# Attention by pairs of heads, one per half of the partitions, and no zero matmuls in any attention stage of a two-block kernel

## The chip, the cores and the metric

The kernel runs on one core of one Trainium2 chip. The metric is the device time of one execution, in microseconds (us). Everything is float32; weights and activations of the large products are split into a high and a low part (type fp32r), and each product is three matmuls.

## The reference

Two blocks over a sequence of 256 tokens and width 1024 (`D_MODEL`). The first: swiglu FFN, short convolution, FFN, shared keys and values, FFN, sparse attention (`nsa_mixer`), FFN. The second: an even mixer and an odd mixer. The three attention stages that the change touches:

```
# nsa: 16 heads of 64, in 4 groups; three branches per head
s_c = q @ k_c.T * scale + bias        # 15 compressed keys
p_c = masked_softmax(s_c); o_c = p_c @ v_c
s_s, o_s = ...  # selected blocks: with 256 tokens all 4 blocks are selected
s_w, o_w = ...  # window of 512: all causal keys
out = g0 * o_c + g1 * o_s + g2 * o_w; return out @ w_o
# even: 8 heads of 64 over the 64 best keys of each query (dsa_attention), beside 4 heads of retention
# odd: 4 differential heads (softmax map 1 minus lambda times map 2, 64 wide each, values 128 wide),
#      a norm over their output, beside 8 latent heads (keys 96 wide, values 64 wide)
```

## The kernel before, in words

The activations lie transposed, feature by token: `qT[:, i]` has the queries of heads 2i (partitions 0 to 63) and 2i+1 (partitions 64 to 127) for 256 tokens. An attention stage is a list of *maps*, one per head and branch. A full map is 128 x 384: queries 128 to 255 against all 256 keys in columns 0 to 255, queries 0 to 127 against 128 keys in columns 256 to 383. A compressed map ("cmp") is 128 x 30. The list of nsa has 48 maps, for each pair of heads three of the lower head, then three of the upper one; even has 8, odd 16.

`attend(name)` stands once per engine, and the copies meet by semaphores. In step `st`:
- TensorE (lines 821 to 877) makes the scores of map `st` into one of three banks (L834, L835; L838, L839 for cmp), transposes map `st - LAG` once it is scaled (L852 to L854), and multiplies map `st - LAG - 1` with the values (L870, L871; L873 for cmp), with `LAG = 5`. In nsa, `fill=2` adds two matmuls of zeros to each step, 128 x 512, into a bank that nobody reads (L876).
- VectorE adds the bias (L1722), takes the row maxima (L1724, L1725), and, one step later, inverts the sums of the exponentials (L1739), applies the gates (L1740) and scales a third of the map (L1745). When a tile of the output is complete, it evacuates it and splits it into `hnh` and `hnl` (L1562, L1563).
- ScalarE copies the transposed map out (L1314) and makes the exponentials with their sums (L1325).
- GpSimd scales the other 256 columns (L2139). In nsa it also loads the diagonals of the bias for the next pair.

`NP_ = 7` maps may be in flight. Each stage is followed by the output projection `mix_out`: 8 chunks of 24 matmuls (L643 to L645), one per tile, after its opening (L656) and a wait for the last tile (`mix_ready`). Its weight chunks pass through a ring of two: SP loads one when the low part of the chunk two before is done, ScalarE makes the high part (`hi_b`, L1114), and the low part is made by GpSimd for chunks 0 and 1 (`lo_b`, L2067), ahead of `attend`, and by VectorE for the others (`mix_rest`, L1767), behind it.

Ahead of nsa, `project("q")` makes the queries in four chunks of 256 columns and the gates in a last chunk of 48. Each chunk of queries is normed: squares on ScalarE, sums on TensorE (L606), root on ScalarE (L1147), `normed_queries` on VectorE (L1491, a reciprocal of 128 x 512, and L1847). In the odd stage the differential heads are normed in the same way (`c_norm`: L1491, L2036, L2037, L1562, L1563), each pair of tiles at a step chosen by `C_DONE`. The nsa stage has its own step counts: the bias diagonals of a pair are awaited by VectorE at its first map.

Of the kernel before, what the change touches and what calls it, by code (L numbers as in the profile page):

```python
# [17 lines left out]
F32 = mybir.dt.float32  # L18
# [7 lines left out]
P = 128  # L26
T = 256
# [5 lines left out]
NP_ = 7  # L33
LAG = 5
# [67 lines left out]
def build(nc, a, out):  # L102
    ctx = ExitStack()
    with ctx:
# [48 lines left out]
        pbuf = sb("pbuf", [P, NP_, 384])  # L153
        ptb = sb("ptb", [P, 2, 384])
        nmx = sb("nmx", [P, NP_, 2])
        sm = sb("sm", [P, NP_, 2])
        rs = sb("rs", [P, NP_, 2])
# [7 lines left out]
        bank = [ctx.enter_context(nc.psum_tensor(f"bank{i}", [P, 512], F32)) for i in range(8)]  # L165
# [139 lines left out]
        Q_COLS = [(T * c, T) for c in range(4)] + [(1024, 48)]  # L305
# [27 lines left out]
        NPAR, NGAIN = len(PARAMS), 6  # L333

# [6 lines left out]
        def _(sp):  # L341
# [65 lines left out]
            def load_rows(w):  # L407
                v = kmaj(w)
                for c in range(KT):
# [22 lines left out]
            load_rows(a["attn_w_o"][0])  # L432
# [5 lines left out]
            load_rows(a["w_out_even_2"][0])  # L438
            load_cols(odd_w, ODD_COLS)
            load_rows(a["w_out_odd_2"][0])  # L440
# [28 lines left out]
        def special(chunk, parts, moves):  # L469
# [5 lines left out]
            "q": [fm(c, qT[:, 2 * c:2 * c + 2]) for c in range(4)] + [nat(4, 0, 48, gates[:, :, :], ACT.Sigmoid)],  # L475
# [44 lines left out]
        def full(q, k, bias, scale, v, rows, coef=None):  # L520
            return dict(kind="full", q=q, k=k, bias=bias, scale=scale, v=v, rows=rows, coef=coef)

        def nsa_units():
            units = []
            for pair in range(8):
                maps = []
                for h in (2 * pair, 2 * pair + 1):
                    half, g = 64 * (h % 2), h // 4
                    r = slice(half, half + 64)
                    q = qT[r, pair]  # L530
                    maps.append(dict(kind="cmp", q=q, k=kcT[r, g * NC:(g + 1) * NC],
                                     bias=tcmp[:, :].rearrange("p (i n h) -> p h i n", i=2, h=16)[:, h],
                                     scale=SQRT_D, v=vc[:, g * 64:(g + 1) * 64], rows=(half, 64),
                                     coef=gates[:, :, 3 * h]))
                    for br in range(2):
                        src = kT if (g % 2) * 64 == half else kS
                        maps.append(full(q, src[r, 2 * br + g // 2], t384[:, pair % 2, h % 2, :], SQRT_D,
                                         [vn[:, br, t, g * 64:(g + 1) * 64] for t in range(2)], (half, 64),
                                         coef=gates[:, :, 3 * h + 1 + br]))
                units.append((maps, pair, None))  # L540
            return units

        def even_units():
            units = []
            for pair in range(4):
                maps = []
                for h in (2 * pair, 2 * pair + 1):
                    half = 64 * (h % 2)
                    r = slice(half, half + 64)
                    maps.append(full(eq[r, pair], ek[r, pair], dmask, SQRT_D,  # L550
                                     [ev[:, t, h * 64:(h + 1) * 64] for t in range(2)], (half, 64)))
                units.append((maps, pair, eg[:, pair]))
            return units

        def odd_units():
            units = []
# [1623 lines left out]
```

## Time and profile before

| | us |
|---|---|
| median of 3 runs | 1516.56 (1515.64 to 1526.63) |
| profiled execution, time | 1513.4 |
| its span | 1511.2 |
| mean granted clock of TensorE | 0.951 of 2.4 GHz |
| busy: TensorE, VectorE, ScalarE, GpSimd | 1402.4, 911.8, 629.7, 438.7 |

The span is what the profile shows from the first to the last instruction of the execution, 2.2 us less than its time. The busy time of an engine is the time in which at least one of its instructions was under way. In the timeline an fp32 matmul shows as two records (x2), whose modelled ends overlap the next instruction; the start-to-start distance is what it costs.

### The profile page before, as it was taken

The numbers are of one execution on the slowest core, as the hardware profiler recorded it, in microseconds if no ns is written. First come the engines' busy times: TensorE is split into PE (matmuls) and PEld (weight loads), VectorE is DVE, ScalarE is ACT, GpSimd is POOL, SyncE is SP. The second block draws the span as 40 slices with busy tenths as digits, with TensorE's granted clock in tenths as the row PEclk, the third lists the DMA queues.
The fourth block names the chain that finished last, engine by engine and source line by source line (L and its number), as shares of the span: only waits on it lengthen the run. The fifth ranks groups of instructions, "written<-read, shape, count | busy, mean of one in ns | idle before, by whom it ended". The sixth has DMA issues, their size and how long they took to land.

```text
span 1511.2 us, 27677 instructions
## 1 busy us (share of the span) xinstructions
PE 1402.4 (93%) x10817; PEld 1288.6 (85%) x10817; DVE 911.8 (60%) x1424; ACT 629.7 (42%) x953; POOL 438.7 (29%) x226
## 2 busy tenths in 40 slices
PE   5999999989999999999979999999999979799766
PEld 4999999989999989999955557899999977688646
DVE  3685468875455665454665664745557695573764
ACT  3344343344334454343434553533443443434442
POOL 1344431214443253434114440344330012000310
PEclk8999999999999999999977999999999997899788
DMA  7768745658766466565430002665644531353002
GB/s 203 216 187 239 213 127 176 189 161 243 217 187 193 127 188 207 178 196 167 130 113 21 22 22 74 206 194 183 206 139 129 165 128 47 105 164 112 28 1 84
DMA packets 271772, 222.53 MB, mean 147 GB/s; under 512 B 8082, under 2 KB 252326, under 8 KB 271580
## 3 DMA queue, kind: packets, MB, share of 16 engines
q1 hardware_dynamic: 268176, 212.44, 46.3%
q0 software_dynamic: 2368, 7.60, 2.2%
q10 hardware_dynamic: 1164, 1.62, 0.3%
q8 instruction: 42, 0.69, 0.2%
q14 instruction: 22, 0.18, 0.0%
HBM read 216.40 MB, written 4.19 MB: 146 GB/s over the span
## 4 chain that ended last, share of the span: by engine, by line
PE 76%; DVE 14%; ACT 5%; DMA 3%; issue 2%; ACTq 0%; DVEq 0%; SPq 0%
PE bank L643 21%; PE bank L645 20%; PE bank L644 20%; DVE wal L1509 2%; PE bank L834 2%; PE bank L876 2%; PE bank L870 2%; DVE rstd L1491 2%; ACT wah L1107 1%; DVE hnl L1527 1%; PE bank L852 1%; ACT hnh L1175 1%; DVE wal L1683 1%; PE bank L835 1%; DMA raw_a<-in_ffn_w_in 1%
## 5 line engine op out<-in xcount | busy, mean ns | idle before, releaser
L643 PE MATMUL bank<-hnh,wah 128*128 128x256 f32 (+1 forms) x2080 | 590.8, 284 | 12.5 <-DVE wal L1509 5.7
L2067 POOL TENSOR_TENSOR wbl<-raw_b,wbh 128x1024 fp32r<-128x1024 f32 x102 | 338.7, 3322 | 878.6 <-ACT wbh L1114 765.2
L644 PE MATMUL bank<-hnl,wah 128*128 128x256 f32 (+1 forms) x2080 | 582.9, 280 | 0.0
L645 PE MATMUL bank<-hnh,wal 128*128 128x256 f32 (+1 forms) x2080 | 582.4, 280 | 0.0
L643 PEld LDWEIGHTS bank<-hnh,wah 128*128 128x128 f32 (+1 forms) x2080 | 397.4, 191 | 18.9 <-issue 10.4
L644 PEld LDWEIGHTS bank<-hnl,wah 128*128 128x128 f32 (+1 forms) x2080 | 395.9, 190 | 2.0 <-issue 1.4
L645 PEld LDWEIGHTS bank<-hnh,wal 128*128 128x128 f32 (+1 forms) x2080 | 396.2, 190 | 0.0
L1509 DVE TENSOR_TENSOR wal<-raw_a,wah 128x2048 fp32r<-128x2048 f32 (+1 forms) x129 | 298.2, 2312 | 95.0 <-ACT wah L1107 93.6
L1107 ACT ACTIVATE wah<-raw_a 128x2048 fp32r<-128x2048 f32 (+3 forms) x127 | 238.9, 1884 | 98.5 <-PE bank L645 80.7
L643 PE MATMUL bank<-hidh,wbh 128*128 128x256 f32 x768 | 214.6, 279 | 4.6 <-DVE hidl L1563 4.5
L1213 ACT ACTIVATE gate_hid<-tmp 128x256 f32<-128x256 f32 x88 | 36.7, 417 | 429.3 <-DVE tmp L1618 429.3
L644 PE MATMUL bank<-hidl,wbh 128*128 128x256 f32 x768 | 214.1, 279 | 0.0
L645 PE MATMUL bank<-hidh,wbl 128*128 128x256 f32 x768 | 214.0, 279 | 0.0
L1618 DVE TENSOR_TENSOR tmp<-bank,rms 128x512 f32<-128x512 f32 x88 | 60.8, 691 | 221.7 <-PE bank L645 214.3
L643 PEld LDWEIGHTS bank<-hidh,wbh 128*128 128x128 f32 x768 | 146.0, 190 | 5.3 <-DVE hidl L1563 4.9
L1114 ACT ACTIVATE wbh<-raw_b 128x1024 fp32r<-128x1024 f32 x120 | 125.2, 1046 | 60.2 <-PE bank L645 37.2
L645 PEld LDWEIGHTS bank<-hidh,wbl 128*128 128x128 f32 x768 | 145.4, 189 | 0.0
L644 PEld LDWEIGHTS bank<-hidl,wbh 128*128 128x128 f32 x768 | 145.3, 189 | 0.0
L2139 POOL TENSOR_SCALAR pbuf<-pbuf,rs 128x256 f32<-128x256 f32 (+1 forms) x72 | 63.9, 887 | 87.4 <-DVE rs L1740 63.0
L1325 ACT ACTIVATE pbuf<-pbuf,nmx 128x128 f32<-128x128 f32 (+2 forms) x144 | 59.4, 413 | 41.6 <-DVE nmx L1725 35.8
L1622 DVE TENSOR_TENSOR gate_hid<-gate_hid,tmp 128x256 f32<-128x256 f32 x88 | 39.5, 448 | 42.7 <-ACT gate_hid L1213 42.7
L834 PE MATMUL bank<-arena 64*128 64x256 f32 (+1 forms) x112 | 46.6, 528 | 18.0 <-DVEq L1968 8.4
(245 smaller groups left out, 1758.7 us busy)
## 6 DMA issues: line engine op xcount, KB each, us to landing
raw_a<-in_ffn_w_in SPq DMA_DIRECT2D x176, 512.0 KB, 5.1
raw_b<-in_ffn_w_out SPq DMA_DIRECT2D x88, 512.0 KB, 4.8
raw_a<-in_w_in_even SPq DMA_DIRECT2D x15, 1024.0 KB, 5.3
raw_a<-in_conv_w_in SPq DMA_DIRECT2D x24, 512.0 KB, 4.2
raw_a<-in_w_in_odd SPq DMA_DIRECT2D x11, 1024.0 KB, 5.3
raw_a<-in_w_kv SPq DMA_DIRECT2D x6, 1024.0 KB, 5.8
raw_b<-in_conv_w_out SPq DMA_DIRECT2D x8, 512.0 KB, 5.8
raw_a<-in_attn_w_q SPq DMA_DIRECT2D x4, 1024.0 KB, 5.3
```

The costliest lines, as they stand in the source:

```text
L643: mm(dst, wh, xh, start=start, stop=False)
L644: mm(dst, wh, xl, start=False, stop=False)
L645: return mm(dst, wl, xh, start=False, stop=stop)
L834: mm(b[:, 0:T], m["q"][:, P:T], m["k"], start=True, stop=True)
L1107: act.activation(wah[:, s, :, 0:w], raw_a[:, wa.slot(u), :, 0:w], ACT.Copy).then_inc(S("a_hi"), 1)
L1114: act.activation(wbh[:, s], raw_b[:, s], ACT.Copy).then_inc(S("b_hi"), 1)
L1325: x = act.activation(pbuf[:, r, lo:hi], pbuf[:, r, lo:hi], ACT.Exp, bias=nmx[:, r, i:i + 1], accum_out=sm[:, r, i:i + 1])
L1509: v.tensor_tensor(wal[:, s, :, 0:w], raw_a[:, (n["ra"] + u) % 2, :, 0:w], wah[:, s, :, 0:w].bitcast(F32), ALU.subtract).then_inc(S("a_lo"), 1)
L1618: v.tensor_tensor(tmp[:, gs, :].rearrange("p (g c) -> p g c", g=2), bank[4 + gs][:, :].rearrange("p (g c) -> p g c", g=2), rln[:, None, :] ...
L1622: link(v.tensor_tensor(hf[:, hs, :], silu[:, gs, :], tmp[:, gs, T:2 * T], ALU.mult))
L2067: g.tensor_tensor(wbl[:, s], raw_b[:, s], wbh[:, s].bitcast(F32), ALU.subtract).then_inc(S("b_lo"), 1)
L2139: g.tensor_scalar(pbuf[:, r, lo:hi], pbuf[:, r, lo:hi], rs[:, r, 1:2], None, ALU.mult).then_inc(S("p1_scaled"), 1)
```

## The change

Two maps of the two heads of a pair become one *duo*, which passes all engines as one step: nsa 24 duos (cmp, full, full per pair of heads), even 4, odd 8. The scores of the two heads go to two neighbouring banks, alternating between the halves of the partitions (in the odd stage's differential heads the two halves are the two maps of one head; the latent heads have 96 partitions each, from 0 on). VectorE and ScalarE handle both maps in one instruction where they can, by a view over two banks; ScalarE's exponentials and GpSimd's scaling stay one per map. Values of a duo alternate between the halves of the output's partitions. At most 3 duos are in flight, and `LAG` is 2.

The two zero matmuls per step are gone. The gates' chunk of `project("q")` moves from last to second. The norms of the last two query chunks move into the nsa stage on VectorE, in halves of 256 columns at steps 2, 4, 6 and 8, with TensorE's sum of the last one at its step 1 and its waits at steps 12 and 18. GpSimd's low parts of chunks 0 and 1 move behind `attend` in all three stages; in nsa ScalarE's two high parts move to its steps 14 and 15. `mix_out` waits for each tile (`tile_ready`) in place of the last one, and takes tiles 4 to 7 first in even and odd. In odd both norms of the differential heads move to VectorE's end: `c_norm(0)` in step 10, `c_norm(1)` behind `attend`, their sums at TensorE's steps 8 and 9.

```diff
-NP_ = 7
-LAG = 5
+ND = 3
+LAG = 2
...
+def two_banks(i, rows, w):
+    return psum[0:rows, 512 * i:512 * (i + 2)].rearrange("p (b c) -> p b c", b=2)[:, :, 0:w]
-Q_COLS = [(T * c, T) for c in range(4)] + [(1024, 48)]
+Q_COLS = [(0, T), (1024, 48)] + [(T * c, T) for c in range(1, 4)]
+OUT_ORDER = {"nsa": list(range(8)), "even": [4, 5, 6, 7, 0, 1, 2, 3], "odd": [4, 5, 6, 7, 0, 1, 2, 3]}
+TILE_COUNT = {"nsa": {c: c + 1 for c in range(8)}, "even": {c: 8 + c + 1 for c in range(4)},
+              "odd": {4: 13, 5: 14, 6: 15, 0: 16, 1: 16, 7: 17, 2: 18, 3: 18}}
@@ TensorE @@
-    def mix_out():
+    def mix_out(name):
+        pe.wait_ge(S("rt_ready"), n["rn"])
         open_acc()
+        for i, c in enumerate(OUT_ORDER[name]):
+            if c in TILE_COUNT[name]:
+                pe.wait_ge(S("tile_ready"), TILE_COUNT[name][c])
+            add_rows(i // 2, i % 2, hnh[:, c, :], hnl[:, c, :], KT)
...
+                x0 = 2 * (g % 2)
+                if g >= 2:
+                    pe.wait_ge(S("max_ready"), g - 1)
+                if du["kind"] == "full":
+                    for i in range(2):
+                        mm(bank[x0 + i][:, 0:T], q[i][:, P:T], k[i], start=True, stop=True)
+                    for i in range(2):
+                        x = mm(bank[x0 + i][:, T:384], q[i][:, 0:P], k[i][:, 0:P], start=True, stop=True)
...
+                if du["kind"] == "full":
+                    pe.wait_ge(S("p1_scaled"), fulls(name, j))
+                if g >= 1:
+                    pe.wait_ge(S("pt_copied"), g)
+                for i in range(2):
+                    p, b = pbuf[:, 2 * (g % ND) + i], bank[6 + i]
+                    if du["kind"] == "full":
+                        pe.transpose(b[:, 0:P], p[:, T:384], ident)
...
+                elif rows[0] == rows[1]:
+                    for i in range(2):
+                        mm(o[:, 0:T], v_[i][0], pt[i][:, 0:T], start=i == 0, stop=False)
+                        x = mm(o[:, P:T], v_[i][1], pt[i][:, T:384], start=False, stop=i == 1)
                 else:
+                    for i in range(2):
+                        mm(o[rows[i], 0:T], v_[i][0], pt[i][:, 0:T], start=first, stop=False)
+                    for i in range(2):
+                        x = mm(o[rows[i], P:T], v_[i][1], pt[i][:, T:384], start=False, stop=last)
-                    for _ in range(fill):
-                        mm(bank[6][:, :], zero[:, 0:P], zero[:, :], start=True, stop=True)
...
-    attend("nsa", fill=2)
-    pe.wait_ge(S("mix_ready"), 1)
-    mix_out()
+    def nsa_between(st):
+        if st == 1:
+            sum_squares(1, 512, blk1)
+        elif st == 2:
+            pe.wait_ge(S("rt_ready"), n["rn"])
+        elif st in (12, 18):
+            pe.wait_ge(S("late_queries"), st // 6 - 1)
...
+    def sum_heads(st):
+        if st in (8, 9):
+            pe.wait_ge(S("max_ready"), DBASE["odd"] + 7)
+            sum_squares(1, 512, one1, (sqs[:, :], tmp[:, 0, :])[st - 8], bank[st - 8])
@@ ScalarE @@
-    take_root(512, 1.0 / 64)
-    mix_first()
-    attend("nsa")
+    take_root(512, 1.0 / 64, sqs, 1)
+    attend("nsa", lambda st: hi_b(0, st - 14) if st in (14, 15) else None)
@@ VectorE @@
+                if du["kind"] == "full":
+                    link(v.scalar_tensor_tensor(pbuf[:, r, :], two_banks(x0, P, 384), du["scale"], du["bias"],
                                                 ALU.mult, ALU.add))
+                    v.reduce_max(nmx[:, r, 1], pbuf[:, r, 0:T], AX, negate=True)
+                    v.reduce_max(nmx[:, r, 0], pbuf[:, r, T:384], AX, negate=True).then_inc(S("max_ready"), 1)
...
+                    split(hnh[:, tile, :], hnl[:, tile, :], dst).then_inc(S("tile_ready"), 1)
...
+    def late_queries(st):
+        if st in (2, 4, 6, 8):
+            j, t = 1 + (st + 2) // 4, (st // 2 + 1) % 2
...
+            link(v.reciprocal(rstd[:, 0:T], (rt if j == 2 else sqs)[:, t * T:(t + 1) * T]))
+            x = v.scalar_tensor_tensor(qT[:, 2 * j + t, :], qT[:, 2 * j + t, :], gq[:, 0:1], rstd[:, 0:T],
+                                       ALU.mult, ALU.mult)
...
+    attend("odd", behind=lambda st: c_norm(0) if st == 10 else None)
+    c_norm(1)
@@ GpSimd @@
+            if du["kind"] == "cmp":
+                if 1 <= du["unit"] < 7:
+                    diagonals(du["unit"] + 1)
+                continue
+            for r in (2 * (g_ % ND), 2 * (g_ % ND) + 1):
+                x = g.tensor_scalar(pbuf[:, r, 0:T], pbuf[:, r, 0:T], rs[:, r, 1:2], None, ALU.mult)
+            x.then_inc(S("p1_scaled"), 1)
     def mix(name):
+        attend(name)
         for u in range(2):
             lo_b(0, u)
-        attend(name)
```

## Rows read from the trace of the kernel before

**Rows 1.** The page's chain of work that ended last, by engine.
```profile
PE 76%; DVE 14%; ACT 5%; DMA 3%; issue 2%; ACTq 0%; DVEq 0%; SPq 0%
```

**Rows 2.** Stretches: length, busy us of PE, PEld, DVE, ACT, POOL; PEclk; DMA share.
```profile
774.90:788.70 13.80, 4.25 (x6) 1.10 (x5) 10.28 (x5) 6.84 (x9) 4.64 (x2) 0.50 0.12 39
788.70:811.40 22.70, 22.70 (x62) 12.00 (x62) 10.48 (x42) 8.15 (x35) 5.82 (x8) 0.50 0.07 23
811.40:918.70 107.30, 106.53 (x529) 58.53 (x527) 65.80 (x254) 54.26 (x205) 42.44 (x53) 1.00 0.08 23
1245.10:1265.20 20.10, 19.25 (x60) 12.97 (x61) 15.30 (x44) 9.71 (x37) 10.13 (x9) 0.50 0.17 53
1428.50:1449.50 21.00, 16.52 (x98) 13.35 (x97) 17.14 (x44) 14.07 (x42) 7.55 (x8) 0.99 0.00 0
```

**Rows 3.** Timeline of PE in nsa: start, length, line, forms, count [idle before].
```profile
844.79 0.61 PE L876 MATMUL bank<-zero 128*128 128x512 bf16 x2
845.33 0.70 PE L834 MATMUL bank<-arena 64*128 64x256 f32 x2
...
846.17 0.33 PE L852 MATMUL bank<-cst,pbuf 128*128 128x128 f32 x1
...
846.65 0.65 PE L870 MATMUL bank<-ptb,arena 128*64 128x256 f32 x2
847.13 0.38 PE L871 MATMUL bank<-ptb,arena 128*64 128x128 f32 x2
847.45 0.60 PE L876 MATMUL bank<-zero 128*128 128x512 bf16 x2
...
852.61 0.70 PE L834 MATMUL bank<-arena 64*128 64x256 f32 x2
```

**Rows 4.** Timeline of PE, first scores of even and of odd.
```profile
1245.12 1.23 PE L834 MATMUL bank<-arena 64*128 64x256 f32 x4 [8.45 <-DVEq L1968]
1246.10 0.68 PE L835 MATMUL bank<-arena 64*128 64x128 f32 x4
...
1412.26 1.23 PE L834 MATMUL bank<-arena 64*128 64x256 f32 x4 [7.96 <-DVEq L2024]
```

**Rows 5.** Timeline of PE, last value products of even.
```profile
1269.34 0.38 PE L871 MATMUL bank<-ptb,arena 128*64 128x128 f32 x2
1269.51 0.65 PE L870 MATMUL bank<-ptb,arena 128*64 128x256 f32 x2
```

**Rows 6.** Timeline of the other engines in nsa.
```profile
824.42 0.56 DVE L1722 SCALAR_TENSOR_TENSOR pbuf<-bank,t 128x384 f32<-128x384 f32 x1 [0.30 <-PE bank L835]
825.01 0.42 DVE L1724 TENSOR_REDUCE nmx<-pbuf 128x1 f32<-128x256 f32 x1
825.35 0.28 DVE L1725 TENSOR_REDUCE nmx<-pbuf 128x1 f32<-128x128 f32 x1
825.54 0.16 DVE L1739 RECIPROCAL rs<-sm 128x2 f32<-128x2 f32 x1
...
828.32 0.51 ACT L1325 ACTIVATE pbuf<-pbuf,nmx 128x256 f32<-128x256 f32 x1 [0.54 <-DVE nmx L1725]
828.64 1.02 POOL L2139 TENSOR_SCALAR pbuf<-pbuf,rs 128x256 f32<-128x256 f32 x1 [0.58 <-DVE rs L1740]
```

**Rows 7.** Timeline ahead of nsa.
```profile
785.74 2.58 DVE L1847 SCALAR_TENSOR_TENSOR arena<-arena,par,rstd 128x512 f32<-128x512 f32 x1
...
788.70 0.60 PE L838 MATMUL bank<-kcT,arena 64*128 64x15 f32 x2 [8.26 <-DVEq L1862]
```

**Rows 8.** Timeline around the openings of the output projections of nsa and odd.
```profile
918.69 1.04 PE L656 MATMUL bank<-zero 128*128 128x512 bf16 x4 [0.77 <-DVE hnl L1563]
...
1458.29 3.35 DVE L1491 RECIPROCAL rstd<-rt 128x512 f32<-128x512 f32 x1 [0.19 <-ACT rt L1147]
...
1464.38 0.42 DVE L1756 TENSOR_TENSOR arena<-bank,arena 128x256 f32<-128x256 f32 x1
...
1466.76 1.89 PE L656 MATMUL bank<-zero 128*128 128x512 bf16 x4 [5.29 <-DVE hnl L1563]
```

More of the change, by code:

```diff
@@ L513, in wait_finished, with nsa_duos @@
                 eng.wait_ge(S("job_finished"), BY_ACT[jobs])
[L520 to L524, printed above, removed]
+        def nsa_duos():
+            duos = []
             for pair in range(8):
[L526 to L541, printed above, removed]
@@ new lines, in nsa_duos @@
+                for br in range(2):
+                    src = [kT if (g % 2) == half else kS for half in range(2)]
+                    duos.append(dict(kind="full", q=q, k=[src[i][rows[i], 2 * br + g // 2] for i in range(2)],
+                                     bias=t384[:, pair % 2, :, :], scale=SQRT_D,
+                                     v=[[vn[:, br, t, g * 64:(g + 1) * 64] for t in range(2)]] * 2, rows=rows,
+                                     coef=gate[1 + br], first=False, last=br == 1, **tile))
@@ new lines, in nsa_duos, with even_duos @@
+            return duos
+        def even_duos():
+            duos = []
+            rows = [slice(0, 64), slice(64, P)]
+            for pair in range(4):
+                duos.append(dict(kind="full", q=[eq[r, pair] for r in rows], k=[ek[r, pair] for r in rows],
+                                 bias=dmask[:, None, :].to_broadcast([P, 2, 384]), scale=SQRT_D,
+                                 v=[[ev[:, t, h * 64:(h + 1) * 64] for t in range(2)] for h in (2 * pair, 2 * pair + 1)],
+                                 rows=rows, coef=None, first=True, last=True, tile=pair, unit=pair, gate=eg[:, pair]))
+            return duos
@@ L562, in odd_units @@
             for pair in range(4):
-                maps = []
-                for h in (2 * pair, 2 * pair + 1):
-                    maps.append(full(q96[0:96, h], k96[0:96, h], causal, 96 ** -0.5,
-                                     [mv[:, t, h * 64:(h + 1) * 64] for t in range(2)], (64 * (h % 2), 64)))
-                units.append((maps, 4 + pair, dg[:, pair]))
-            return units
-        STAGES = {"nsa": nsa_units(), "even": even_units(), "odd": odd_units()}
-        C_DONE = 8 + LAG + 1
@@ L572, in build @@
[L572 to L587 removed]
+                hs = (2 * pair, 2 * pair + 1)
@@ new lines, in odd_duos @@
+                duos.append(dict(kind="full", q=[q96[0:96, h] for h in hs], k=[k96[0:96, h] for h in hs], bias=bias,
+                                 scale=96 ** -0.5, v=[[mv[:, t, h * 64:(h + 1) * 64] for t in range(2)] for h in hs],
+                                 rows=rows, coef=None, first=True, last=True, tile=4 + pair, unit=4 + pair,
+                                 gate=dg[:, pair]))
+            return duos
+        STAGES = {"nsa": nsa_duos(), "even": even_duos(), "odd": odd_duos()}
@@ L866, in attend @@
+                        o, v_, first, last = bank[4 + gu % 2], du["v"], du["first"], du["last"]
+                        pt = [ptb[:, 2 * (g % 2) + i] for i in range(2)]
                         pe.wait_ge(S("pt_copied"), g + 1)
```

347 lines of the change are left out of this document (167 added, 180 removed).

## The prediction, made before the change was run

> **What bounds the kernel now.** I read the chain that ended last first: TensorE holds 76% of it, VectorE 14% [rows 1]. Then the busy time by stretches, for the clock and for how full TensorE is around the three attention stages [rows 2]. In the first one (nsa, 8 pairs of heads, 48 maps) TensorE is busy 106.5 of 107.3 us, always at the full 2.4 GHz, while VectorE, ScalarE and GpSimd have 66, 54 and 42 us of work there. So the stage is as long as TensorE's instruction stream. Before it stand 13.8 us with little on TensorE and 22.7 us at half clock (1.2 GHz), in which every record of it is twice as long. The timeline gives the stream's parts, start to start [rows 3]: the scores of a full map 0.84 us (845.33 to 846.17), three transposes 0.48, the two value products 0.80, the two zero matmuls 0.54 (844.79 to 845.33). Three steps (one compressed map, two full ones) repeat after 7.28 us (845.33 to 852.61), a pair of heads after 14.57, eight pairs after 116.6. The zero matmuls are 6 x 0.54 = 3.2 us of each pair, 26 us of the stage.
>
> **What the change takes off TensorE.** Zero matmuls: those 3.2 us per pair. Scores of a pair: one head has partitions 0 to 63, the other 64 to 127, and two maps on different halves do run side by side: at the start of the even stage four records of 256 columns and four of 128 belong to two maps and take 1245.12 to 1246.78, 1.66 us at half clock [rows 2, 4], where two maps one after the other would need 4 x 0.84 = 3.4. So a pair's scores cost 0.84 at full clock; in the last four units of the odd stage, with 96 partitions, they stay at 1.68. Value products of a pair: the heads write different halves of the output's partitions. The trace has one place where such products follow each other with nothing between: the second product of one head starts at 1269.34 and the first of the next head at 1269.51 [rows 5], 0.17 later, where inside the nsa stage the next instruction comes 0.32 after it (847.13 to 847.45) [rows 3]. They overlapped, so I take 0.8 for a pair; the other end is 1.6, nothing shared. The Trainium skill, "TensorE: Matmul & The Clock Gate", section "Measured speedup vs the span model", has 2.38 times for three column tiles; by that a pair would take about 0.9 to 1.0 (an estimate from that page). The row agrees in kind. Transposes use the whole array and stay, 0.96 per pair.
>
> **What is late next.** TensorE's work per nsa pair falls to about 2.2 (scores) + 2.5 (transposes) + 2.2 (values) = 6.9 us. What sets the pace then is a ring through all engines, since only three pairs of maps are in flight (ND = 3, LAG = 2) where seven maps were. Its other terms [rows 6]: on VectorE one map takes 0.56 + 0.42 + 0.28, 1.12 to the reciprocal's start; doubling the elements from 128 to 256 costs 0.14, so a fixed 0.14 of each operation is saved by handling two maps at once: 0.98 + 0.70 + 0.42, less the overlap that these operations show, 1.92 for a pair. Reciprocal and multiplication about 0.37. GpSimd scales 256 columns in 1.02, twice: 2.04. ScalarE: four exponentials, about 1.84.
> Over one unit (three steps) TensorE's program order and the waits close this ring: transposes 0.96, values 0.80, scores 0.84, VectorE's scores-to-maximum 1.92, factor 0.37, GpSimd 2.04, transposes 0.96, values of the compressed maps 0.57 (estimated between 0.48 and 0.80 [rows 3]), scores 0.84. Sum 9.3, and 0.3 for three or four hand-overs: 9.6 us per pair of heads, against 14.57. Eight: 77. The new waits are these: TensorE waits for GpSimd's scaling with the next values and scores queued behind it, and VectorE waits behind those scores with the factors of the maps before.
>
> **Stage by stage,** on the profiled execution (span 1511.2, time 1513.4):
> - Gap before nsa. The projection ends where the first stretch begins [rows 2], 774.9, and the first score is at 788.70 [rows 7], behind two query norms on VectorE and a blocked one: 2.58 us at 785.74, while GpSimd made a low part. The last two norms move into the stage as eight small operations (about 8.6 us on VectorE, which has room) and GpSimd's work moves to its end. Left: one sum of squares, an evacuation, about 2.3 us. The 48-column chunk moves from last to second; the clock was already at half where it ended [rows 2], and now full-width matmuls follow it: 1.7 lost. First score at 778.9.
> - nsa. First scores and their root 2 us, 77, then the drain of the last pair: maximum 1.9, exponentials 1.8, factor, GpSimd 2.0, transposes 1.0, the copy of 768 columns 0.9 (estimated), values 0.8, hand-overs: 9.7; opening the banks 0.9. That is 90. The start-up has holes of 4 to 5 us on TensorE, after which I expect half clock until the pipe is full: 5 us. First product of the output projection at 873, where it was about 0.7 behind the opening at 918.69 [rows 8], 919.4. Gain 46.
> - even. Four pairs are hardly a pipe: the last scores about 9 behind the first, drain 9.7: 19 us at full clock, 23 at half; it starts cold again, so 21.5, against 25.2 (1245.12 to 1270.3) [rows 4, 5]. The wait of about 0.8 ahead of the mix [rows 8] goes, and GpSimd no longer blocks VectorE at the start, about 1.8. Gain 6.
> - odd. Without compressed maps the ring closes over two steps: 0.96 + 1.6 (values of full width share nothing) + 0.84 + 1.92 + 0.37 + 2.04 = 7.7, later 7.8 (values 0.8, scores 1.68), with hand-overs 4.1 a pair. Last scores at 28, drain 9.7: 38, cold start plus 4: 42, against 49.2 (1412.26 [rows 4] to 1466.76 less 5.29 idle [rows 8]). Then both head norms, 6.1 us each (1458.29 to 1464.38 [rows 8]), stand on VectorE behind the last evacuations, ahead of the low parts of chunks 2 to 7. The mix starts at once with two chunks (5.4 us) and then waits about 8, where it waited 5.3 ahead; and the clock may drop: 1.5. Gain 7 - 2.7 - 1.5 = 3.
> - Moved loads. SP may refill a weight buffer only behind GpSimd's low part, now at the end of each stage. GpSimd makes the first one (4.64 us for two [rows 2], 2.3) while TensorE does the last transposes and values (about 3), so I cost it at nothing; if VectorE's port use stretches these to 3.5, each stage gives back up to 1 to 3 us.
> Sum: 46 + 6 + 3 = 55 to 56. 1513.4 - 55.7 = 1457.7. The median of the runs shown, 1516.56, is 3.2 above the profiled execution; most of that I expect again: **1460**.
>
> **The rivals.**
> 1. *Half clock through nsa.* For it: the even stage stayed at 0.50 for 20 us with TensorE busy 19.25 of 20.10, and without zero matmuls; nsa took 22.7 us to reach full clock even with them [rows 2]. Against: from 1428.5 to 1449.5 the odd stage holds 0.99 with TensorE busy only 79%, no zero matmuls in it. The ring's TensorE terms double, 4.97 to 9.9, and a unit takes 9.6 + 5.0 = 14.6, as long as now: 8 x 5.0 = 40 less the 5 already in. 1495, and up to 1507 if the odd stage stays cold too.
> 2. *The value products do not overlap.* For it: one place only shows overlap. The ring gets 0.8 + 0.57 longer, 11.0 a unit: 11 us in nsa, 2 or 3 in the others. 1473.
> 3. *Slower than before.* Both at once: value products one after the other and half clock. TensorE alone then needs 2 x (2.2 + 2.5 + 4.3) = 18 us per pair, where the forecast has 9.6: 8 x 8.4 = 67, less the 5 already in, and about 12 in the other two stages: 1534. It turns slower than before where a pair passes about 16.
> 4. *Scores do not pair up in the steady stage,* because transposes and values stand between: of the two places that show the overlap neither is in such a step [rows 4]. 2 x 0.84 a unit more, and 2 us in even and odd each: about 1475.
> 5. *VectorE alone sets the pace,* the ring's waits being hidden. Its work in a unit is 2 x (1.92 + 0.37 + 0.45 for scaling) + 1.0 for the compressed maps + 1.2 for the output tile, both estimated from operations of that size [rows 6]: 7.7 against the ring's 9.6. Eight units are 15 us less: 1445. The Trainium skill, "TensorEngine Tiling (Array Packing)", section "PSUM Bottleneck", says that tiling speeds up TensorE but not the emptying of PSUM, which may then be the bound. By that rule it would be this case; the rows have VectorE at 66 us of 107 [rows 2], and no more than 62 of the 77 to come.
>
> **How the numbers follow.** Forecast 0.58 (own range 1446 to 1473), half clock 0.2, rival 2 0.09, rival 4 0.03, slower 0.06, rival 5 0.04. The range reaches from 1441 to 1497, which leaves out the slow case and the far end of rival 1. Faster by over 1% (15 us, about what a measurement here can tell from no change): 0.90. Within 1%: 0.04. Slower: 0.06.
>
> **What would show it.** A period of 9.6 us between the first scores of two pairs in nsa; score records of two heads with starts closer than 0.2 us, and value records likewise; TensorE waiting for GpSimd's scaling as its largest wait in the stage, not VectorE; a gap of 2 to 3 us ahead of nsa; in the odd mix a hole of about 8 us after two chunks, released by VectorE. Granted clock 1.0 in most of nsa. Wrong would make it: 0.50 there, one of the rings through ScalarE (copy of 768 columns ahead of the exponentials) being longer than mine, or diagonals that land late (3.2 us, now asked for three steps ahead of use, not six).

## The result, and the profile after

| kernel | time, us (median; lowest to highest) | profiled execution, its span |
|---|---|---|
| before | 1516.1 (1515.4 to 1526.6) | 1513.4, 1511.2 |
| after | 1465.6 (1459.9 to 1472.9) | 1472.9, 1471.2 |

The ratio is 0.9649, with a 95% interval of 0.9603 to 0.9695: 50.5 us less, where 56 were forecast. The profiled execution of after is the longest of its four, 40.5 us under that of before, and the difference by stages says why. Each mark is a start in TensorE's timeline: last product of a projection, first score, opening of the banks, the zero matmul that closes a product. The *mix* is the output projection behind an attention stage.

| stage, us | before | after | difference |
|---|---|---|---|
| start to the end of the first feed-forward | 215.7 | 220.6 | +5.0 |
| convolution | 97.4 | 96.8 | -0.6 |
| second feed-forward | 187.4 | 192.8 | +5.5 |
| keys and values, third feed-forward | 240.7 | 239.3 | -1.4 |
| query projection | 33.6 | 37.9 | +4.3 |
| wait before the first score of nsa | 13.9 | 1.8 | -12.1 |
| nsa, first score to the opening of the mix | 130.0 | 102.9 | -27.1 |
| its output projection, fourth feed-forward, even projection | 317.7 | 318.8 | +1.1 |
| even: wait, attention, mix | 60.3 | 52.4 | -7.9 |
| odd projection and tail | 125.7 | 126.4 | +0.7 |
| odd: wait, attention, mix | 88.9 | 81.4 | -7.5 |

The query projection, the wait, nsa, even and odd together gave 50.3 us. The output projection of nsa, whose low parts the change moves too, is 0.8 us longer (24.7 against 24.0). The +10.5 in two feed-forwards is not the change's work: in a feed-forward the matmuls start either every 0.113 or every 0.118 us (355 or 342 in 40 us), from its first to its last. Stretches of before and of after, with the columns of [rows 2]:
```profile
60.00:100.00 40.00, 40.00 (x355) 40.00 (x354) 31.35 (x41) 14.76 (x18) 18.89 (x8) 1.00 0.72 213
```
```profile
60.00:100.00 40.00, 40.00 (x342) 40.00 (x341) 32.09 (x43) 15.74 (x18) 18.86 (x8) 1.00 0.73 217
```
Granted clock and busy time are the same. Over the 14 profiles of this study the first feed-forward has the slow pitch in 7, the second in 4, the third in all 14 (before too), the fourth in 2. A slow one is longer by about 6 us (6.1, 6.6 and 6.5 on average in the first, second and fourth), so the time of one execution moves by that much without any edit; below, stage lengths are compared beside the medians.

Stretches of after; the first, seventh and eighth answer to [rows 2], the second to fifth are pieces of a single pair of heads:
```profile
789.30:892.20 102.90, 75.04 (x483) 50.36 (x485) 71.04 (x182) 59.98 (x222) 43.94 (x46) 0.73 0.09 25
836.00:840.00 4.00, 1.45 (x18) 1.21 (x17) 3.33 (x13) 1.86 (x8) 2.72 (x3) 1.00 0.22 86
840.00:846.80 6.80, 6.80 (x35) 4.44 (x34) 3.39 (x9) 4.52 (x18) 2.67 (x4) 0.50 0.04 7
846.80:850.30 3.50, 2.15 (x24) 1.33 (x22) 3.08 (x8) 1.73 (x6) 0.79 (x1) 0.99 0.42 104
850.30:857.00 6.70, 5.49 (x24) 3.75 (x24) 3.67 (x10) 4.57 (x15) 3.13 (x4) 0.50 0.00 0
764.00:772.00 8.00, 8.00 (x40) 8.00 (x40) 3.10 (x3) 4.82 (x7) 0.00 (x0) 0.51 0.22 78
1217.60:1238.60 21.00, 15.12 (x88) 11.02 (x90) 15.21 (x31) 11.86 (x38) 11.53 (x10) 0.64 0.03 5
1379.70:1416.30 36.60, 29.45 (x181) 23.17 (x183) 28.29 (x62) 25.78 (x79) 18.43 (x18) 0.86 0.00 1
```
Here the granted clock goes up and down within each pair: 1.00 for some 4 us, 0.50 for some 6.8, then 0.99, then 0.50. Before, once it was up it stayed at 1.00 to the end of nsa. The fifth, sixth and seventh pair take 12.3, 11.7 and 12.3 us between first scores, not 9.6. The timeline of TensorE through one of them answers to [rows 3]:
```profile
833.80 0.70 PE L846 MATMUL psum<-arena 64*128 64x256 f32 x4
834.34 0.39 PE L848 MATMUL psum<-arena 64*128 64x128 f32 x4
834.65 0.28 PE L870 MATMUL psum<-cst,pbuf 128*15 128x128 f32 x1
...
835.19 0.65 PE L892 MATMUL psum<-ptb,arena 128*64 128x256 f32 x4
835.68 0.39 PE L894 MATMUL psum<-ptb,arena 128*64 128x128 f32 x4
836.00 0.62 PE L852 MATMUL psum<-kcT,arena 64*128 64x15 f32 x8
839.17 0.30 PE L866 MATMUL psum<-cst,pbuf 128*128 128x128 f32 x1 [2.55 <-issue]
...
840.93 1.23 PE L846 MATMUL psum<-arena 64*128 64x256 f32 x4
```
Scores of two heads take 0.85 us from start to start (833.80 to 834.65), values of two 0.81 (835.19 to 836.00). Then TensorE is idle for 2.55 us, and 0.8 us after it resumes its records are twice as long. What it waits for, in the waits of TensorE in nsa (us, times, longest):
```profile
PE psum L866 <- issue: 16.5, 7, 2.6
PE psum L866 <- POOL pbuf L2195: 8.8, 3, 5.0
```
"Issue" stands here where TensorE awaited several semaphores (`pt_copied`, `p0_scaled`, `p1_scaled`). GpSimd's two scalings of the duo end at 839.07, and TensorE goes on at 839.17. The timeline of GpSimd:
```profile
837.17 1.90 POOL L2195 TENSOR_SCALAR pbuf<-pbuf,rs 128x256 f32<-128x256 f32 x2 [1.64 <-DVE rs L1773]
```

In the odd stage's output projection, timeline of TensorE, then of VectorE, then of GpSimd:
```profile
1433.98 0.55 PE L651 MATMUL psum<-hnh,wbh 128*128 128x256 f32 x1 [11.24 <-DVE wbl L1807]
```
```profile
1413.48 2.29 DVE L1592 CAST hnh<-arena 128x256 fp32r<-128x256 f32 x1
1415.80 2.47 DVE L1593 TENSOR_TENSOR hnl<-arena,hnh 128x256 fp32r<-128x256 f32 x1
...
1418.64 0.29 DVE L1592 CAST hnh<-arena 128x256 fp32r<-128x256 f32 x1
1418.97 0.43 DVE L1593 TENSOR_TENSOR hnl<-arena,hnh 128x256 fp32r<-128x256 f32 x1
1419.32 3.35 DVE L2085 RECIPROCAL rstd<-rt 128x512 f32<-128x512 f32 x1
...
1426.52 3.35 DVE L2085 RECIPROCAL rstd<-sqs 128x512 f32<-128x512 f32 x1
...
1432.61 2.35 DVE L1807 TENSOR_TENSOR wbl<-raw_b,wbh 128x1024 fp32r<-128x1024 f32 x2
```
```profile
1413.26 4.73 POOL L2122 TENSOR_TENSOR wbl<-raw_b,wbh 128x1024 fp32r<-128x1024 f32 x2
```
The hole is there, 11.2 us. The first two rows of VectorE are a split that takes 0.29 and 0.43 a little later (1418.64); they lie beside GpSimd's two low parts. Beside GpSimd's scalings, which read one tile and not two, the same cast takes 0.30 and the same subtraction 0.50 (nine times in this trace). The kernel before has one such case too: 2.57 and 2.72 us from 1242.22 on, ahead of its even stage.

### The profile page after: what moved, and what is told of

It is laid out like the page before. It is cut to its first block, busy times and chain, and to the rows that moved or that the text cites. A ratio compares the mean times of both kernels' runs of the same rounds, so it can differ in the third digit from the quotient of the medians.

```text
span 1471.2 us, 27135 instructions
## 1 busy us (share of the span) xinstructions
PE 1336.7 (91%) x10692; PEld 1268.2 (86%) x10709; DVE 895.5 (61%) x1260; ACT 617.9 (42%) x915; POOL 428.7 (29%) x210
## 4 chain that ended last, share of the span: by engine, by line
PE 73%; DVE 15%; ACT 5%; issue 3%; DMA 3%; POOL 0%; ACTq 0%; DVEq 0%; SPq 0%; POOLq 0%
PE psum L651 22%; PE psum L653 21%; PE psum L652 21%; DVE wal L1539 2%; PE psum L846 1%; ACT wah L1136 1%; ACT hnh L1206 1%; DVE pbuf L1751 1%; PE psum L866 1%; DVE hnl L1557 1%; DVE wal L1713 1%; DMA raw_a<-in_ffn_w_in 1%; DVE rstd L1521 1%; PE psum L627 1%; DVE rms L1529 1%
## 5 line engine op out<-in xcount | busy, mean ns | idle before, releaser
L651 PE MATMUL psum<-hnh,wah 128*128 128x256 f32 (+1 forms) x2080 | 593.4, 285 | 32.1 <-DVE hnl L1557 13.5
L652 PE MATMUL psum<-hnl,wah 128*128 128x256 f32 (+1 forms) x2080 | 585.0, 281 | 0.0
L653 PE MATMUL psum<-hnh,wal 128*128 128x256 f32 (+1 forms) x2080 | 584.6, 281 | 0.0
L651 PEld LDWEIGHTS psum<-hnh,wah 128*128 128x128 f32 (+1 forms) x2080 | 396.4, 191 | 19.5 <-issue 11.5
L653 PEld LDWEIGHTS psum<-hnh,wal 128*128 128x128 f32 (+1 forms) x2080 | 397.8, 191 | 0.0
L652 PEld LDWEIGHTS psum<-hnl,wah 128*128 128x128 f32 (+1 forms) x2080 | 395.1, 190 | 2.2 <-issue 1.7
L1136 ACT ACTIVATE wah<-raw_a 128x2048 fp32r<-128x2048 f32 (+2 forms) x127 | 238.7, 1882 | 92.9 <-PE psum L653 68.1
L651 PE MATMUL psum<-hidh,wbh 128*128 128x256 f32 x768 | 215.6, 281 | 5.3 <-DVE hidl L1593 5.3
L653 PE MATMUL psum<-hidh,wbl 128*128 128x256 f32 x768 | 215.3, 280 | 0.0
L652 PE MATMUL psum<-hidl,wbh 128*128 128x256 f32 x768 | 215.3, 280 | 0.0
L651 PE MATMUL psum<-hnh,wbh 128*128 128x256 f32 x192 | 55.7, 290 | 13.7 <-DVE wbl L1807 13.6
```

The lines of the kernel that those rows point to most:

```text
L651: mm(dst, wh, xh, start=start, stop=False)
L652: mm(dst, wh, xl, start=False, stop=False)
L653: return mm(dst, wl, xh, start=False, stop=stop)
L1136: act.activation(wah[:, s, :, 0:w], raw_a[:, wa.slot(u), :, 0:w], ACT.Copy).then_inc(S("a_hi"), 1)
```

## The experiments

All start from the kernel after, but e8. "nsa" is the stretch from its first score to the opening of its mix, as in the table. Behind each median stands the ratio to the kernel before, which ran again beside each group of runs with medians from 1512.1 to 1519.0. So a gain over after is a little uncertain where it is taken from medians of different groups: e1, e2 and e12 are 23, 20 and 33 us below 1465.6 by the medians, but some 20, 15 and 29 by the ratios.

**e1: four duos in flight.**
```
-ND = 3, LAG = 2
+ND = 4, LAG = 3      # the fourth place lies in gate_hid, or tmp in the even stage
```


> One more duo in flight in every attention stage: four places for probabilities in place of three, and transposes three steps behind the scores in place of two. The first theory (each unit of the first stage is held by a ring: exponentials, reciprocal, GpSimd's 2 us of scaling, transposes, ScalarE's copy, and ScalarE's next exponentials stand behind that copy) expects the 2.6 us wait of TensorE in each unit to vanish, the granted clock to stay at full and the unit to fall from 12 us to 8 to 9 us: 20 to 28 us less than the changed kernel's 1465.6, so about 1440. The rival that the half clock would come anyway, because TensorE has too little to do between its waits, expects a unit of 11 us or more and under 8 us of gain. The rival that VectorE or GpSimd by itself sets the pace expects no gain.

1442.5 us (1437.2 to 1446.6), ratio 0.9517 (0.9453 to 0.9582). 23 us less, as expected; but nsa gave 16 of them (86.9 us), even 1.2 and odd 5.2. The pairs take 4.8, 14.7, 8.3, 14.9, 6.8, 11.1 and 6.6 us, between first scores. Stretches: nsa, and its first two pairs:
```profile
778.10:865.00 86.90, 67.16 (x482) 44.98 (x484) 70.99 (x182) 59.25 (x222) 44.01 (x46) 0.81 0.11 32
778.10:797.60 19.50, 13.71 (x80) 8.90 (x80) 15.40 (x33) 11.82 (x47) 5.05 (x6) 0.65 0.00 1
```
The ring was a cause. That the clock would stay full did not come true: 0.81 on average.

**e2: zero matmuls where TensorE waits.**
```
 pe.wait_ge(S("pt_copied"), g)   # stood behind the other waits; now ahead of the zeros
+for _ in range(20):          # nsa, ahead of the second duo's transposes
+    mm(bank[6][:, T:2 * T], zero[:, 0:P], zero[:, 0:T], start=True, stop=True)
 pe.wait_ge(S("p0_scaled"), g + 1)
```


> Twenty zero matmuls of 256 columns (2.1 us at full clock) put where TensorE waits longest in each unit of the first stage, ahead of the transposes of the second duo of three; nothing else is changed. The first theory (that wait is what takes the clock to half for some 6.5 us of each 12 us unit) expects full clock through the stage, a unit of 9.5 to 10.3 us and 12 to 18 us off 1465.6. The rival that the clock's dips have another cause expects them to stay, and the time unchanged or longer by up to 2 us a unit.

1445.7 us (1438.7 to 1454.4), 0.9548 (0.9481 to 0.9616). nsa 86.4. Stretches of this run: nsa, then the fifth and the sixth pair:
```profile
776.50:862.90 86.40, 77.59 (x642) 55.04 (x644) 70.51 (x182) 60.12 (x222) 42.94 (x46) 0.94 0.10 29
818.20:827.40 9.20, 8.92 (x82) 6.51 (x80) 7.81 (x23) 6.95 (x28) 5.37 (x7) 1.00 0.14 43
827.40:836.70 9.30, 9.02 (x84) 6.57 (x82) 7.91 (x24) 8.69 (x30) 5.46 (x7) 1.00 0.20 45
```
With the same ring, and only zeros added to the work, the last pairs have full clock and take 9.2 us each. So the zeros gave 16.5 us of nsa back, and what they changed is the clock: 0.94 on average against 0.73. The second, third and fourth pair, beside VectorE's late query norms, took 12.8, 12.1 and 10.1.

**e3: both.**
```
 e1, and range(6) ahead of the transposes of both full duos
```


> Both together: four duos in flight, and six zero matmuls of 256 columns ahead of the transposes of each full duo of the first stage. If the longer ring alone ends the wait and the dips, this is no faster than it and up to 8 us slower (12 x 0.107 us in each of 8 units at most 10 us of work). If the dips stay with the longer ring alone, this one takes them away, and comes out 5 to 15 us ahead of it.

1443.2 us (1442.2 to 1448.2), 0.9511 (0.945 to 0.9571); nsa 88.6 at a clock of 0.85. That is no gain over e1, so the 5 to 15 us expected for the case that e1's dips stay did not come. Three late pairs take 7.8, 9.3 and 7.8 us at full clock, but the two in which VectorE has late query norms 16.2 and 15.6. The last two of the three, and the last alone:
```profile
836.30:853.40 17.10, 15.68 (x147) 11.50 (x144) 15.39 (x44) 15.45 (x57) 10.60 (x12) 1.00 0.16 43
845.60:853.40 7.80, 7.80 (x74) 5.75 (x72) 6.96 (x22) 6.93 (x28) 5.30 (x6) 1.00 0.09 17
```
In the pair of 7.8 us TensorE is busy all the time, 1.3 us of it with twelve zero matmuls (an estimate from 12 x 0.107 us), while VectorE and ScalarE are busy for 6.9 to 7.0. The same pair in e1, without zeros:
```profile
838.70:845.30 6.60, 6.60 (x62) 4.66 (x62) 5.76 (x18) 5.83 (x27) 5.04 (x6) 1.00 0.01 2
```
There too TensorE is busy all the time and the clock is full, so in these pairs the zeros cost what they take. Over the three pairs little changes, 24.5 us in e1 (6.8, 11.1, 6.6) and 24.9 here: the pair in between, whose clock in e1 is 0.85, gains what its neighbours lose.

**e4: the order within a pair.**
```
-for i in range(2): mm(... [:, 0:T] ...)      # 256 columns of both heads
-for i in range(2): mm(... [:, T:384] ...)    # then 128 of both
+for i in range(2): mm(...); mm(...)          # one head, then the other; values too
```


> The same matmuls as in the changed kernel, but each head's two score matmuls one after the other, then the other head's, and the same for the values, so that no two of different halves follow each other but at the change of head. The theory that the two halves overlap (a pair of scores in 0.85 us, a pair of values in 0.81 us, where one after the other they would take some 1.5 us each) expects each duo to take 1.3 us more of TensorE, 28 full duos 36 us in all, of which what TensorE's waits now hide is given back: 10 to 30 us slower than 1465.6. The rival that overlap brings nothing because the ring sets the pace expects under 5 us.

1460.5 us (1455.5 to 1476.4), 0.961 (0.9547 to 0.9672): no difference from after. It was no test of the overlap. Timeline of TensorE, this run:
```profile
841.01 0.71 PE L846 MATMUL psum<-arena 64*128 64x256 f32 x4
841.55 0.39 PE L847 MATMUL psum<-arena 64*128 64x128 f32 x4
841.87 0.28 PE L869 MATMUL psum<-cst,pbuf 128*15 128x128 f32 x1
```
Issued as 256, 128, 256, 128 columns, they still ran as both 256 and then both 128, in 0.86 us (the first two rows are four records each; the first of the two heads start 0.013 us apart): the second head starts beside the first even if another matmul of the first stands ahead of it in the kernel. The trace does not show where on the way from the kernel to the engine the order changes. The Trainium skill, "TensorE: Matmul & The Clock Gate", section "The mechanism", has matmuls start strictly in program order; by that only the first head's matmul of 128 columns and the second head's of 256 could lie side by side, and the scores of a duo would take some 1.4 us (an estimate from the rows: 0.54 + 0.54 + 0.32). The row differs, and it decides.

**e5: the heads' scores held apart.**
```
 for i in range(2):
+    if i: mm(bank[x0][:, 384:392], zero[:, 0:P], zero[:, 0:8], start=True, stop=True)
     mm(...); x = mm(...)
```


> The heads' scores held apart: both matmuls of the first head, a zero matmul over all 128 rows with 8 columns, then both of the second head. In the run with the order changed alone the second head's first matmul still started 0.013 us after the first head's, so the order had undone nothing; the full-row matmul should. The theory that pairs are worth their overlap expects a duo's scores to take some 1.75 us in place of 0.85 at full clock, in all three stages, and the time 8 to 22 us over 1465.6 (20 to 28 us if none of it is hidden by waits). The rival that TensorE's waits hide it expects under 4 us.

1502.4 us (1493.3 to 1508.5), 0.9884 (0.9802 to 0.9965): 37 us over after by the medians (36 by the ratios), more than either end. Timeline, at half clock:
```profile
855.48 1.22 PE L848 MATMUL psum<-arena 64*128 64x256 f32 x2
856.50 0.63 PE L849 MATMUL psum<-arena 64*128 64x128 f32 x2
857.06 0.19 PE L847 MATMUL psum<-zero 128*128 128x8 bf16 x1
857.18 1.22 PE L848 MATMUL psum<-arena 64*128 64x256 f32 x2
858.20 0.63 PE L849 MATMUL psum<-arena 64*128 64x128 f32 x2
858.76 0.47 PE L867 MATMUL psum<-cst,pbuf 128*128 128x128 f32 x1
```
3.28 us for a duo, 1.64 at full clock against 0.85. For 16 full duos that is 12.6 us, but nsa grew by 25.2 (to 128.1), and the clock's mean there fell from 0.73 to 0.62. The attention of even grew by 3.3, that of odd by 3.5. So without the overlap the stage has more to do on TensorE and a lower clock besides. What the values' overlap is worth no run shows.

**e6: the normalisations further back.**
```
-attend("odd", behind=c_norm(0) at step 10); c_norm(1); mix_rest()
+attend("odd"); mix_rest with c_norm(0) behind chunk 2, c_norm(1) behind chunk 4
```


> The last stage's two normalisations of the differential heads moved behind the third and the fifth chunk of the output weights on VectorE, in place of ahead of all of them; the same work. The theory that the 11.2 us hole in the last output projection is VectorE's queue (two normalisations of 6.1 us ahead of the third chunk's low half) expects the hole to fall to two of 2 to 4 us, the projection from 36.6 us to 29 to 33, and the time 4 to 7 us under 1465.6. The rival that the hole comes from the transfer or from ScalarE's high half expects it to stay.

1453.9 us (1451.8 to 1455.2), 0.9566 (0.95 to 0.9632); by the profiles the odd mix went from 36.6 to 30.8. What is left of the hole, timeline of TensorE:
```profile
1418.00 0.36 PE L651 MATMUL psum<-hnh,wbh 128*128 128x256 f32 x1 [4.15 <-DVE wbl L1809]
...
1426.36 0.36 PE L651 MATMUL psum<-hnh,wbh 128*128 128x256 f32 x1 [0.95 <-DVE wbl L1809]
```
VectorE's queue it was. The mix explains 5.8 us of the 11.7 by which the median is below 1465.6, where 4 to 7 were expected; the rest has no counterpart in the stages that the edit touches.

**e7: the gates' 48 columns last.**
```
-Q_COLS = [(0, T), (1024, 48)] + [(T * c, T) for c in range(1, 4)]
+Q_COLS = [(T * c, T) for c in range(4)] + [(1024, 48)]
```


> The 48 columns of the gates back in the last place of the query projection. The theory that the chunk in second place costs by the clock (about 8 us of half clock in the projection, 36 to 38 us against 33.6 before) expects the projection 2 to 4 us shorter, the first scores' wait 1 to 3 us longer (sigmoid and gates are then late) and the half clock carried into the first steps of the attention: the time within 3 us of 1465.6 either way. If the wait before the first scores goes back to 8 us or more, the place of the chunk was what shortened it.

1459.9 us (1454.5 to 1466.7), 0.9599 (0.953 to 0.9667), 5.7 us under after, where at most 3 were expected; the ranges overlap, so the medians alone do not tell the two apart. The projection took 33.6 us, the wait before the first score 2.2, nsa 103.0. Over all profiles: 36.2 to 37.9 with the chunk in second place (8 of them), 33.3 to 34.2 with it last (6). Its place costs 2 to 4.6 us, and of the shorter wait at most 0.4 us hangs on it.

**e8: before, without its zero matmuls.**
```
-attend("nsa", fill=2)
+attend("nsa")
```


> The kernel before, with the two zero matmuls of each step of its first attention stage left out and nothing else. The theory that the fill kept the clock up in the changed kernel's twelve-microsecond units too, and that its removal cost there, expects here as well dips of the granted clock wherever TensorE waits over 2 us. In the kernel before the engine waits little between its steps (14.6 us a unit, TensorE busy), so the likeliest is a gain of 5 to 20 us over 1516 from the removed work (48 steps x 2 x 0.21 us); if the clock falls to half for good parts of the stage, it is slower by up to 20 us.

1547.3 us (1541.9 to 1550.5), 1.0177 (1.0102 to 1.0251): slower by 34 than the kernel before as it ran beside it (1513.5). nsa took 162.5 us, against 130.0. Stretches of nsa in this run:
```profile
795.40:957.90 162.50, 161.02 (x481) 96.81 (x482) 75.97 (x296) 61.21 (x240) 48.33 (x60) 0.51 0.07 18
840.00:850.00 10.00, 10.00 (x30) 5.94 (x30) 5.01 (x20) 3.52 (x15) 2.54 (x3) 0.50 0.00 0
```
TensorE is busy 161.0 of 162.5 us, with less to do than in [rows 2], and stays at 1.2 GHz until its last few us (0.77 over the last 7.9). Taken alone, the second half of the change is a loss.

**e9: the fill of e2 on a quarter of the array.**
```
+mm(bank[6][0:64, T:2 * T], zero[0:64, 0:64], zero[0:64, 0:T], ...)   # 20 times
```


> The fill of the second run once more, twenty zero matmuls of 256 columns in the same place, but each over 64 rows and 64 columns of the array, a quarter of it, in place of the whole. TensorE is busy for the same time. The theory that the clock follows how long TensorE is busy expects the result of the whole-array fill: full clock, a unit of 9.2 us, about 1446. The theory that work on the whole array is wanted (the kernel before without its zero matmuls was busy 10.0 of 10 us with single heads on half the rows and stood at half clock from end to end) expects the dips of the changed kernel to stay and a unit of 12 us or a little more: 1460 to 1475.

1459.1 us (1458.0 to 1461.8), 0.9627 (0.9568 to 0.9685); nsa 92.7, between after (102.9) and e2 (86.4). Stretches:
```profile
820.00:830.00 10.00, 8.13 (x38) 5.47 (x40) 5.45 (x17) 5.77 (x25) 5.10 (x6) 0.52 0.01 3
840.00:850.00 10.00, 9.66 (x86) 7.21 (x88) 8.61 (x23) 9.40 (x34) 6.17 (x8) 1.00 0.16 41
```
The last pairs run at full clock in 9.2 us as in e2, but a dip stays around 820 to 830 (a pair of 15.4). Neither theory is borne out as it stands: here the clock stayed up in the last pairs but dropped once where e2's had not. One profile does not say more.

**e10 and e11: what helped, together.**
```
 e1 + e3's fill + e6 + e7, and ahead of the scores of steps 4, 6, 8, 10:
+pe.wait_ge(S("pt_copied"), d0 + st - LAG)
+for _ in range({4: 28, 6: 12, 8: 16, 10: 16}[st]): mm(bank[6] ...)
 e11: also 44 and 56 zero matmuls after the even and the odd projection
```


> Four duos in flight, six zero matmuls ahead of each full duo's transposes and 28, 12, 16 and 16 at the four steps that VectorE's late query normalisations delay, the gates' columns last, and the last stage's normalisations behind the third and fifth chunk. If the single gains hold side by side (first stage from 102.9 to about 78 us, now at VectorE's 7.8 us a unit; projection of queries 4 less; odd stage 6 less for the tail, 3 less for the ring, even 1.7), 1465.6 - 25 - 4 - 9 - 2 = about 1426. If the parts give back to each other, or zero matmuls hold up the real ones, 1432 to 1440.

> The same with 44 and 56 zero matmuls of 256 columns in the waits of 6.6 and 8.2 us ahead of the even and the odd stage's first scores. The theory of the clock expects full clock from the first scores in both, where 11 to 14 us now stand at half, and 3 to 4 us less in each stage: 5 to 8 us under the run without them. If VectorE or ScalarE sets the pace of those steps anyway, under 2 us.

1446.5 us (1439.4 to 1448.0), 0.9527 (0.9479 to 0.9574), and 1444.4 (1439.9 to 1449.1), 0.953 (0.9486 to 0.9575): both missed 1426. The zeros in the gaps brought 2.0 us by the medians and nothing by the ratios, as the rival said: the granted clock over the first 11 us of even rose from 0.50 to 0.74, but the attention of even went only from 19.4 to 18.7 us and that of odd from 34.9 to 34.6, and VectorE is busy 10.18 of those 11.00 us. The odd mix and the query projection kept their gains (30.3 to 30.4 and 33.3 to 33.9), nsa did not: 93.2 and 95.1, where e1 alone had 86.9. Timeline of TensorE in e10:
```profile
798.39 5.99 PE L854 MATMUL psum<-zero 128*128 128x256 bf16 x28 [5.97 <-ACT ptb L1362]
```
The first fill stood behind a wait for ScalarE's copy, which itself stands behind exponentials: 6 us of idle time first, by then half clock, and 6 us of zeros ahead of real scores.

**e12: the early fill at a place that waits for nothing.**
```
 e11, the zeros in the gaps included, with
-steps 4, 6, 8, 10: 28, 12, 16, 16, behind pt_copied, into bank 6
+steps 3, 4: 8, 26, into bank 5, no wait; step 10: 8, as before
```


> The last but one run's kernel with its early fill moved: there 28 zero matmuls stood behind a wait for ScalarE's copy and ran at half clock (6.0 us idle and 6.0 us of zeros ahead of the fifth duo's scores, first two units 27 us). Here 8 and 26 go to an output bank that nobody uses yet, ahead of the fourth and fifth duo's scores and behind no wait, and only 8 are left of the later ones. The theory (the zeros' place, not the longer ring, lost the gain) expects full clock through the first two units, these in 17 to 20 us, the first stage in 78 to 86 us against 95, and 1430 to 1438. The rival that VectorE's late normalisations alone set those two units expects them at 20 us or more and 1438 to 1446.

1432.3 us (1429.9 to 1440.1), 0.9458 (0.9418 to 0.9497): the fastest of all, 33 us under the kernel after by the medians. Stretches: nsa, its first two pairs, the fourth, the last three:
```profile
784.70:874.20 89.50, 74.56 (x621) 53.16 (x620) 70.56 (x181) 60.07 (x223) 42.94 (x46) 0.92 0.10 28
784.70:804.20 19.50, 17.61 (x127) 12.59 (x126) 13.59 (x29) 10.69 (x40) 3.75 (x4) 0.81 0.01 2
814.60:831.00 16.40, 10.94 (x84) 7.53 (x82) 12.20 (x29) 8.02 (x32) 6.00 (x7) 0.79 0.16 47
838.90:874.20 35.30, 30.17 (x274) 21.57 (x272) 27.79 (x80) 26.43 (x95) 21.82 (x22) 1.00 0.13 34
```
The first two pairs came down from 27.2 us (e11) to 19.5, and nsa from 95.1 to 89.5, which is half of the 12 us between the two. But e1, with the same ring and no zeros at all, has the same 19.5 us for these pairs, at a clock of 0.65, and a shorter nsa, 86.9. So the early zeros here did no harm any more, and no good that a run shows: with four duos in flight every run with zeros has a longer nsa (88.6 to 95.1) than e1, by one profile each. What puts e12 ahead of e1 by the profiles lies elsewhere: 3.0 us in the query projection, 1.7 in even, 4.4 in odd.

nsa is above the 86 expected. The fourth pair takes 16.4 us, and its eight zeros are the one fill that is still behind a wait of its own:
```profile
822.08 1.89 PE L858 MATMUL psum<-zero 128*128 128x256 bf16 x8 [4.77 <-ACT ptb L1373]
```
That this wait is the cause is not shown: the fourth pair took 15.6 us in e3, which has no zeros there, and 11.5 in e10 and e11, which have sixteen.

## Why the prediction was right, and by how much not

- *Score and value pairs overlap* (0.84 and 0.8): 0.85 and 0.81, in the steady stage too. Rivals 2, 3 and 4 fall. For the values that is less than the 0.9 to 1.0 that I had worked out, as an estimate, from the Trainium skill, "TensorE: Matmul & The Clock Gate", section "Measured speedup vs the span model". e5 shows what the scores' part is worth.
- *The ring of 9.6 us a pair.* Its size was right: 9.2 in e2, where the clock is full; VectorE's part, forecast at 1.92, is 1.92 in after (1403.32 to 1405.24). As run the ring took some 12 us, and this is the step that failed: "after which I expect half clock until the pipe is full: 5 us". The half clock came back in nearly every pair: 0.73 on average, where "Granted clock 1.0 in most of nsa" was the sign named. In e2 nsa is 16.5 us shorter than after; 5 were forecast, so some 11 were missing. The pairs beside the late query norms, for which VectorE was said to have room, took 10.1 to 12.8 us even in e2; its clock had two dips there, so the norms' own cost stays open.
- *Rival 1, half clock through nsa,* was that mechanism in part: 2.5 to 3.1 us a pair over e2's 9.2, not 5.0. My row against it, the odd stage at 0.99 with TensorE busy 79%, did not carry over to nsa. The two differ in more than one way (full-width values in odd, one wait of 2.55 us in each pair of nsa), and which difference counts was not tried. The row that I should have questioned was nsa at 1.00 with its zero matmuls, and what it would be without them: e8 says 0.51.
- *Gap before nsa:* 2.3 forecast, 1.8 measured. *The 48-column chunk:* 1.7 forecast, 4.3 in this profile, 2 to 4.6 over all. The stretch from 764 to 772 shows 0.51 with TensorE busy 8.00 of 8.00. Projection, gap and nsa together gained 34.9 us, forecast 46.
- *Even:* 6 forecast, 7.9 measured: the attention took 21.1 us, forecast 21.5, but the wait ahead of the mix that went was 1.3, not 0.8, and the wait ahead of the first scores fell by 2.1.
- *Odd:* 3 forecast, 7.5 measured. The attention is 17.9 us shorter (12.6 but for the 5.3 us wait that was in it), not 7: the last scores start 25.4 us behind the first, where 28 and 4 for a cold start were forecast. Two terms were too large: the value products of full width, 1.6 a duo, took 1.31 (1396.05 to 1397.36), and the latent heads' scores, 1.68, took 1.31 to 1.46. The mix is 10.4 longer; the hole was to be 8 and was 11.2. VectorE's split beside GpSimd's moved low parts took some 4 us more, and the norms stand behind it: by the timeline that is the difference, though no run took it away. So the "moved loads", costed at nothing, did cost, but by way of VectorE; GpSimd's own parts took 2.4 us each, not 3.5.
- *Rival 5, VectorE at 7.7 us a pair:* not the bound in after. With four places in the ring late pairs take 7.8 us in e3 and e12, near that figure, but there TensorE, with its zeros, is busy all the time and VectorE for 6.96; without zeros such a pair took 6.6 (e1), under the 7.7. Over its three late pairs e1 has VectorE busy 21.1 of 24.5 us, so VectorE may well be the bound there, but that is argued. The Trainium skill, "TensorEngine Tiling (Array Packing)", section "PSUM Bottleneck", says that emptying PSUM may become the bound once tiling has sped up TensorE; no run here isolates that.

The sum: 55.7 forecast, 50.3 by stages, 50.5 by the medians. nsa's clock and the chunk took some 11 to 14 away, the rest of nsa gave some 3 back and the odd and even stages some 6. So 1460 came near in part by luck: errors of opposite sign offset each other.

## What to carry to other kernels

Before you take a fill of zero matmuls out, price it by a run without it: a TensorE that is busy all the time was no proof of a full clock (e8: 161.0 of 162.5 us busy, 0.51). If zeros are put in, they belong inside the wait after which the clock drops, and not behind a long wait of their own: e2 gained 16.5 us in nsa that way, e10 stood 6.0 us idle ahead of its first ones. Shortening the wait itself did as much here: the longer ring without any zeros (e1) gave nsa 16.0 us, and zeros on top of it gave nothing more. Overlap two half-height matmuls by giving them different halves; their order within the pair does not matter, a full-height matmul between them does.

## What the runs showed of the hardware that I had not expected

- A stage of single-head matmuls, on half the rows or half the columns, and transposes, with TensorE busy 161.0 of 162.5 us, ran at 1.2 GHz almost to its end (e8); two zero matmuls of 128x512 in each of its 48 steps were worth 34 us to the kernel before.
- Two matmuls of different row halves start together even when the kernel has a second matmul of the first half between them (e4: 0.86 us for all four, 0.85 in after).
- VectorE's cast and subtraction of 256 columns took 2.29 and 2.47 us beside GpSimd's subtractions of 1024, 0.30 and 0.50 beside its scalings of 256, and 0.29 and 0.43 with nothing beside them.
- A feed-forward runs at one of two pitches, 0.113 or 0.118 us a matmul, at the same granted clock; about 6 us each. What picks it was not tried and stays open, as does what remains of nsa's dips in e12.
